# Expert layers with lists of 32 tokens on four strips of TensorE, and results returned through a DRAM table

## What is computed

```
def hier_moe(x, w_group, b_group, w_expert, b_expert, w1, w3, w2):
    ...
    weight = g_gate * e_gate
    expert_id = g_idx * MOE_EXPERTS_PER_GROUP + e_idx
    gates = jnp.sum(jax.nn.one_hot(expert_id, N_EXPERTS, dtype=f32) * weight[..., None], axis=1)

    def step(acc, ew):
        w1e, w3e, w2e, ge = ew
        h = jax.nn.silu(xt @ w1e) * (xt @ w3e)
        return acc + ge[:, None] * (h @ w2e).astype(f32), None

    y, _ = lax.scan(step, jnp.zeros((t, d), f32), (w1, w3, w2, gates.T))
```

## Time and profile before

| | |
|---|---|
| time, median of three runs | 2823.86 us |
| span of the profiled execution (first to last instruction) | 2819.0 us |
| median less span: what lies around | 4.9 us |
| TensorE busy | 2512.3 us, 89% of the span |
| VectorE, ScalarE, GpSimd busy | 800.3, 628.9, 164.9 us |
| bytes moved by DMA | 602.27 MB, mean 214 GB/s |
| MoE weights among them | 192 DMAs of 2 MB |
| chain that ended last | PE 70%, SP's queue 14%, DVE 6%, DMA 4% |

### The profile page before, as it was taken

One profiled execution on the slowest core, in us unless ns is written; L12 is line 12 of the kernel. 1 busy time (PEld: TensorE's weight loads), 2 busy tenths in 40 slices (PEclk: granted clock), 3 DMA queues, 4 the chain that ended last, 5 costly groups with the idle time before them and its releaser, 6 DMA issues.

```text
span 2819.0 us, 30761 instructions
## 1 busy us (share of the span) xinstructions
PE 2512.3 (89%) x12481; PEld 1598.0 (57%) x12482; DVE 800.3 (28%) x1338; ACT 628.9 (22%) x1012; POOL 164.9 (6%) x90
## 2 busy tenths in 40 slices
PE   7878999999979979999897897898999968878998
PEld 6544444444356644443333785556887847744996
DVE  1252011010020221011002546524232326354444
ACT  1121010101000610111102312423222224224334
POOL 0000000000000000000000325000000004240000
PEclk9988999999989989999999988899999988789999
DMA  8675976999966669999999001300323140130351
GB/s 326 260 276 187 393 286 231 393 393 394 396 250 243 233 242 385 394 393 393 395 396 359 1 1 60 123 1 22 113 90 120 45 163 1 60 117 7 135 199 71
DMA packets 241920, 602.27 MB, mean 214 GB/s; under 512 B 12679, under 2 KB 21751, under 8 KB 241824
## 3 DMA queue, kind: packets, MB, share of 16 engines
q1 hardware_dynamic: 241824, 600.91, 56.7%
HBM read 598.25 MB, written 2.64 MB: 213 GB/s over the span
## 4 chain that ended last, share of the span: by engine, by line
PE 70%; SPq 14%; DVE 6%; DMA 4%; ACT 2%; issue 2%; POOL 1%; DVEq 0%; ACTq 0%; POOLq 0%
PE ps L1756 13%; SPq L647 13%; PE ps L752 10%; PE ps L1565 8%; PE ps L1772 7%; PE ps L759 6%; PE ps L214 4%; PE ps L735 3%; PE ps L727 3%; PE ps L223 3%; PE ps L1738 3%; DMA ring<-in_moe_w_dram 1%; PE ps L1689 1%; PE ps L1709 1%; PE ps L313 1%
## 5 line engine op out<-in xcount | busy, mean ns | idle before, releaser
L752 PE MATMUL ps<-ring,arena 128*64 128x512 f32 x2176 | 477.2, 595 | 20.6 <-DMA ring<-in_moe_w_dram 18.7
L1756 PE MATMUL ps<-ring_r,ring_r 128*128 128x512 f32 (+1 forms) x2112 | 372.1, 339 | 12.5 <-DVE ring_r L2090 12.5
L1756 PEld LDWEIGHTS ps<-ring_r,ring_r 128*128 128x128 f32 x2112 | 329.0, 192 | 54.8 <-DVE ring_r L2090 13.1
L752 PEld LDWEIGHTS ps<-ring,arena 128*64 128x64 f32 x2176 | 155.9, 137 | 335.1 <-issue 305.8
L759 PE MATMUL ps<-ring,arena 128*64 128x512 f32 x1088 | 248.5, 598 | 26.8 <-ACT arena L817 13.8
L1565 PE MATMUL ps<-ring_r,ring_r 128*128 128x512 f32 (+2 forms) x1056 | 217.7, 367 | 8.9 <-DVE ring_r L1975 8.9
L1289 POOL TENSOR_TENSOR ring_r<-ring,ring_r 128x1024 fp32r<-128x1024 f32 (+2 forms) x28 | 85.9, 3088 | 2180.6 <-ACT ring_r L1284 2180.6
L1565 PEld LDWEIGHTS ps<-ring_r,ring_r 128*128 128x128 f32 x1056 | 189.1, 212 | 37.4 <-issue 9.3
L1772 PE MATMUL ps<-ring_r,ring_r 128*128 128x512 f32 x480 | 157.4, 401 | 12.3 <-DVE arena_r L1332 12.3
L759 PEld LDWEIGHTS ps<-ring,arena 128*64 128x64 f32 x1088 | 76.4, 137 | 151.2 <-issue 130.3
L907 DVE TENSOR_TENSOR arena<-ps,arena 128x512 f32<-128x512 f32 x34 | 23.6, 693 | 470.0 <-PE ps L752 470.0
(11 more groups left out here) (321 smaller groups left out, 2500.1 us busy)
## 6 DMA issues: line engine op xcount, KB each, us to landing
ring<-in_moe_w_dram SPq DMA_DIRECT2D x192, 2048.0 KB, 19.3
ring<-in_w_mod_dram SPq DMA_DIRECT2D x24, 2048.0 KB, 13.5
ring<-in_w_gate_dram SPq DMA_DIRECT2D x10, 2048.0 KB, 9.1
ring<-in_w_up_dram SPq DMA_DIRECT2D x10, 2048.0 KB, 14.2
ring<-in_w_in_dram SPq DMA_DIRECT2D x8, 2048.0 KB, 14.8
ring<-in_w_down_dram SPq DMA_DIRECT2D x8, 2048.0 KB, 11.4
ring<-in_w_out_dram SPq DMA_DIRECT2D x4, 2048.0 KB, 10.1
ring<-in_w_down_dram SPq DMA_DIRECT2D x4, 1536.0 KB, 8.1
```

The lines of the kernel that those rows point to most:

```text
L752: ins = pe.matmul(PS[CAP * e:CAP * e + CAP, 2 + c, :], xeT[:, k, CAP * e:CAP * e + CAP], w[c][:, e, k, :], start=(k == 0), stop=(k == KT - 1))
L1756: ins = pe.matmul(PS[:, 2 * (i % GU_BANKS) + a, 0:ntok], w[:, k, a, :], as_r(x[:, k, 0:ntok]), start=(k == 0 and n == 0), stop=(k == KT - ...
```

## The change

- CAP goes from 64 to 32 tokens of an expert in a round. In the up products each expert takes two strips of 32 columns of the array: one strip for the left half of the hidden width (`HALF` = 256 columns), one for the right. In the down product the two strips of an expert take the left and right 512 columns of the output. The loads of weights from DRAM are the same.
- Per round, PE's `scatter`, the transposes and copies of `selg`, and the product with the gates are gone. A round's result, 128 rows of 512 values (four strips: expert and half), is copied by DVE to `Y`, and ACT's queue sends it to a block of a table `y_rows` in DRAM, 256 KB a round (262,144 bytes). DVE's next copy to Y waits until this store has landed (`y_sent`).
- After the last round GpSimd (POOL) issues eight indirect DMAs a layer, each of 128 rows of 2 KB from the table, by row numbers that DVE has computed (`pick`): for both token tiles, both picks, both halves. DVE then forms wa * first + wb * second in four instructions, and the layer norm reads SBUF instead of PSUM.
- At the start of the program SP's queue writes zeros over the table (ten stores of 1 MB, from the memory of `O`), placed behind the load of da_wo and ahead of the store of the bias table, on whose landing the loads of the modulation weights wait.
- Ahead of the first round DVE computes the row numbers, after `ctrl` is written.

With the lists above, 34 rounds (18 and 16) become 43 (22 and 21): in layer 0 pairs 4, 5 and 6 take 3, 4 and 2 rounds where they took 2, 2 and 1.

The diff, cut to its core:

```diff
+    ROUNDS_MAX = 40
+    y_rows = nc.dram_tensor("y_rows", [ROUNDS_MAX * P, 512], F32)
...
+        sp.wait_ge(S("o_zero"), 1)
+        for n in range(ROUNDS_MAX // 4):
+            sp.dma_start(y_rows.ap()[4 * n * P:4 * (n + 1) * P, :].rearrange("(p a) d -> p (a d)", a=4), view(O[:, 0, 0:1], [1, 2048]))\
+              .then_inc(S("y_zeroed"), 16)
         sp.wait_ge(S("cc1"), 3)
         sp.dma_start(scratch.ap(), tab_sb).then_inc(S("tab_dma"), 16)
         sp.wait_ge(S("tab_dma"), 16)
...
+            if u == 0:
+                act.wait_ge(S("y_zeroed"), 16 * (ROUNDS_MAX // 4))
             act.wait_ge(S("values"), u + 1)
...
-    CAP = 64
+    CAP = 32
+    HALF = HIDDEN // 2
...
+        Yt = (ring[:, 3 * SLOT:3 * SLOT + 4096] if layer else arena[:, MARK:MARK + 4096]).rearrange("p (t n d) -> p t n d", t=NT, n=2)
...
+        cR, cB, cL = 50 * layer, 50 * layer + 16, 50 * layer + 33
...
-                    n_rounds = eng.value_load(ctrl[0:1, bass.ds(it * UNROLL + (cR + j), 1)], min_val=1, max_val=4)
+                    n_rounds = eng.value_load(ctrl[0:1, bass.ds(it * UNROLL + (cR + j), 1)], min_val=1, max_val=SEQ // CAP)
...
-            for b in range(4):
-                ins = pe.matmul(PS[:, 4 + b, :], zeros[:, 0:P], zeros, start=True, stop=False, skip_group_check=True)
-            ins.then_inc(s("sgT_ps"), 1)
-
-            def scatter(last=False):
-                for tt in range(NT):
-                    for h in range(2):
-                        ins = pe.matmul(PS[:, 4 + 2 * tt + h, :], sgT[:, tt * P:(tt + 1) * P], Y[:, h * 512:(h + 1) * 512],
-                                        start=False, stop=last, skip_group_check=True)
-                return ins
...
             def gather():
 
                 for k in range(KT):
                     for tt in range(NT):
-                        ins = pe.matmul(PS[:, 2 + k // 4, (k % 4) * P:(k % 4 + 1) * P], X[:, tt, k * P:(k + 1) * P],
-                                        view(sel[:, tt, 0, 0:1], [1, P]), start=(tt == 0), stop=(tt == NT - 1))
-                    if k % 4 == 3:
-                        ins.then_inc(s("xe"), 1)
+                        ins = pe.matmul(PS[:, 2, 2 * CAP * k:2 * CAP * (k + 1)], X[:, tt, k * P:(k + 1) * P],
+                                        view(sel[:, tt, 0, 0:1], [1, 2 * CAP]), start=(tt == 0), stop=(tt == NT - 1))
+                ins.then_inc(s("xe"), 1)
...
                         for e in range(2):
-                            ins = pe.matmul(PS[CAP * e:CAP * e + CAP, 2 + c, :], xeT[:, k, CAP * e:CAP * e + CAP], w[c][:, e, k, :],
-                                            start=(k == 0), stop=(k == KT - 1))
+                            for o in range(2):
+                                at = 64 * e + 32 * o
+                                ins = pe.matmul(PS[at:at + CAP, 2 + c, 0:HALF], xeT[:, k, CAP * e:CAP * e + CAP],
+                                                w[c][:, e, k, o * HALF:(o + 1) * HALF], start=(k == 0), stop=(k == KT - 1))
...
-                def down(h):
+                def down():
                     for k in range(4):
                         for e in range(2):
-                            ins = pe.matmul(PS[CAP * e:CAP * e + CAP, h, :], hT[:, k, CAP * e:CAP * e + CAP],
-                                            w[2][:, e, k, h * 512:(h + 1) * 512], start=(k == 0), stop=(k == 3))
+                            for o in range(2):
+                                at = 64 * e + 32 * o
+                                mid = 64 * e + 32 * (k // 2)
+                                ins = pe.matmul(PS[at:at + CAP, 0, :], hT[:, k % 2, mid:mid + CAP],
+                                                w[2][:, e, k, o * 512:(o + 1) * 512], start=(k == 0), stop=(k == 3))
                     return ins
...
-                pe.wait_ge(s("xe_act"), g + 1)
-                pe.wait_ge(s("xe_dve"), g + 1)
+                pe.wait_ge(s("xe_sb"), g + 1)
                 up(0)
                 up(1)
-                pe.wait_ge(s("y_act"), g + (1 + layer))
-                pe.wait_ge(s("y_dve"), g + (1 + layer))
-                scatter()
-                for tt in range(NT):
-                    ins = pe.transpose(PS[:, 0, tt * P:(tt + 1) * P], selg[:, tt, :], ident)
-                ins.then_inc(s("sgT_ps"), 1)
                 pe.wait_ge(s("h"), g + 1)
-                for k in range(4):
+                for k in range(2):
                     ins = pe.transpose(PS[:, 1, k * P:(k + 1) * P], hh[:, k * P:(k + 1) * P], ident)
                 ins.then_inc(s("hT_ps"), 1)
-                pe.wait_ge(s("sgT"), g + (2 + layer))
-                pe.wait_ge(s("hT"), g + 1)
-                arrived(2)
-                down(0)
                 pe.wait_ge(s("sel"), g + (2 + layer))
                 gather()
-                down(1).then_inc(s("y"), 1)
+                pe.wait_ge(s("hT"), g + 1)
+                pe.wait_ge(s("y_sb"), g + (1 + layer))
+                arrived(2)
+                down().then_inc(s("y"), 1)
             pe.wait_ge(s("ctrl"), layer + 1)
-            for b in range(2):
-                ins = pe.matmul(PS[:, b, :], zeros[:, 0:P], zeros, start=True, stop=True)
-            ins.then_inc(s("y"), 1)
+            pe.matmul(PS[:, 0, :], ident, cst[:, 0:512], start=True, stop=True).then_inc(s("y"), 1)
+            if layer == 0:
+                pe.matmul(PS[:, 2, :], ident, cst[:, 0:512], start=True, stop=True).then_inc(s("xe"), 1)
...
-            pe.wait_ge(s("y_act"), total + (1 + layer))
-            pe.wait_ge(s("y_dve"), total + (1 + layer))
-            scatter(last=True).then_inc(s("done"), 1)
+            pe.wait_ge(s("y_sb"), total + (1 + layer))
...
+            if layer == 0:
+                act.dma_start(y_rows.ap()[(ROUNDS_MAX - 1) * P:ROUNDS_MAX * P, :], cst[:, 0:512]).then_inc(s("y_sent"), 16)
...
-                act.wait_ge(s("xe"), g * 2 + (2 * layer + 1))
-                act.copy(view(xeT[:, 0, 0:1], [1, 512]), PS[:, 2, :]).then_inc(s("xe_act"), 1)
-                y_copy(g)
+                act.wait_ge(s("xe"), g + (layer + 2))
+                act.copy(view(xeT[:, 0, 0:1], [1, 512]), PS[:, 2, :]).then_inc(s("xe_sb"), 1)
+                at = act.value_load(ctrl[0:1, bass.ds(it * UNROLL + (cL + j), 1)], min_val=0, max_val=31 * P)
+                act.wait_ge(s("y_sb"), g + (1 + layer))
+                act.dma_start(y_rows.ap()[bass.ds(r * P + at, P), :], Y).then_inc(s("y_sent"), 16)
                 act.wait_ge(s("h1"), g + 1)
-                act.activation(hs, PS[:, 2, :], ACT.Silu).then_inc(s("silu"), 1)
-                act.wait_ge(s("sgT_ps"), g + (2 + layer))
-                act.copy(sgT, PS[:, 0, 0:256]).then_inc(s("sgT"), 1)
+                act.activation(hs, PS[:, 2, 0:HALF], ACT.Silu).then_inc(s("silu"), 1)
...
-                act.copy(view(hT[:, 0, 0:1], [1, 512]), PS[:, 1, :]).then_inc(s("hT"), 1)
-
-            def y_copy(g):
-
-                act.wait_ge(s("y"), g + (1 + layer))
-                act.copy(Y[:, 0:512], PS[:, 0, :]).then_inc(s("y_act"), 1)
+                act.copy(view(hT[:, 0, 0:1], [1, HALF]), PS[:, 1, 0:HALF]).then_inc(s("hT"), 1)
             for_rounds(act, body)
-            y_copy(act.value_load(ctrl[0:1, cB + PAIRS:cB + PAIRS + 1], min_val=1, max_val=128))
+            total = act.value_load(ctrl[0:1, cB + PAIRS:cB + PAIRS + 1], min_val=1, max_val=128)
+            at = act.value_load(ctrl[0:1, cL + PAIRS:cL + PAIRS + 1], min_val=0, max_val=32 * P)
+            act.wait_ge(s("y_sb"), total + (1 + layer))
+            act.dma_start(y_rows.ap()[bass.ds(at, P), :], Y).then_inc(s("y_sent"), 16)
...
-            link(dve.tensor_tensor(oh1, oh1, b2(wa, 32), ALU.mult))
-            link(dve.tensor_tensor(oh2, oh2, b2(wb, 32), ALU.mult))
-            link(dve.tensor_tensor(gates, oh1, oh2, ALU.add))
...
-            dve.tensor_copy(ctrl[:, cB:cB + 17], base).then_inc(s("ctrl"), 1)
+            link(dve.tensor_copy(ctrl[:, cB:cB + 17], base))
+            link(dve.tensor_scalar(blocks, base, base[:, 0:1], float(P), ALU.subtract, ALU.mult))
+            dve.tensor_copy(ctrl[:, cL:cL + 17], blocks).then_inc(s("ctrl"), 1)
+            link(dve.tensor_scalar(slot_of[:, 0:32:2], blocks[:, 0:16], float(P), None, ALU.add))
+            link(dve.tensor_scalar(slot_of[:, 1:32:2], blocks[:, 0:16], float(P + 64), None, ALU.add))
+            for n, oh in enumerate((oh1, oh2)):
+                link(dve.tensor_tensor(where, oh, view(slot_of, [0, NT], [1, 32]), ALU.mult))
+                link(dve.tensor_reduce(place[:, :, n:n + 1], where, AX.X, ALU.add))
+                link(dve.tensor_tensor(where, oh, rank, ALU.mult))
+                link(dve.tensor_reduce(turn[:, :, n:n + 1], where, AX.X, ALU.add))
+            link(dve.tensor_tensor(place, place, turn, ALU.add))
+            for m in range(1, SEQ // CAP):
+                link(dve.tensor_scalar(beyond, turn, m * CAP - 0.5, float(P - CAP), ALU.is_gt, ALU.mult))
```

(38 more changed lines are left out.)

31 lines of the change are left out of this document (12 added, 19 removed).

## The result

The changed kernel takes **2927.9 us**, median of four runs (2920.76 to 2935.03); the kernel before took 2824.58 beside it (2822.52 to 2826.35). The ratio is 1.0372, 95% interval [1.0354, 1.0389]: slower by 103 us. The forecast was slower by 47. The direction was right, but the measured change is more than twice the forecast one. The time lies in the stated range by luck: it is above the forecast's own range (2838 to 2905), which had been widened to 2945 for stores that wait behind the loads, and that is not what happened.

The account below looks back on a forecast made before the run. Weight loads, nearly level with PE, were taken to bound the expert loops. Zeros 11.2, layer 0 15.6 and layer 1 20.7 made 47.5 on a 2819.0 us span; with 4.9 for the median, 2871 us, range 2838 to 2945.

Parts of the forecast that it names:

- the forecast's own range: Whole kernel: 2838 to 2905 us, from varying the round, the gathers and the zeros; the forecast had chance 0.68.
- A pair takes 31.9 us and a faster PE meets a floor 2 us away.: Expert loops: loads need 31.9 us a pair, PE 29.75 a round, so a faster PE wins under 62 us.
- Sum: 16 us a round.: Expert loops: a new round's products, copies and selection add up to 16 us, within 15 to 17.5.
- Layer 0, "last w2 at 780.7": Layer 0's last weight landing: 780.7 against 778.0, with 44.8 us of stalls and 11.3 of Y stores.
- Layer 1, "no pair has over two rounds, so there is no stall": Layer 1's loop: no load stalls, 14.0 us for 21 stores, last w2 at 1522.5 against 1514.7.
- The start of a layer, 4.8 and 4.3: Before the first gather: DVE's added row-number steps delay it 4.8 us in layer 0, 4.3 in layer 1.
- The end of a layer, 12.9 each: Last w2 to layer norm: down, copy, store, gathers (16) and DVE sum to 30.1 us, against 17.2 before.
- The zeros, 11.2: Program start: 10.49 MB of zeros take 25.6 us and make the first modulation product wait 11.2 us.
- The queue rival: Y stores and gathers wait behind weight loads, lengthening layer ends and layer 0's additional rounds: 2945 us; chance 0.12.
- Stores beside loads at no cost: DMA engines: zeros and Y stores cost nothing beside loads, 2834.5 us, faster with short gathers; chance 0.07.
- Clock: PE's clock stays low between waits, also in rounds in a row: 26 us a round, 3016 us; chance 0.04.
- Strips not four abreast: Up and down products: the four strips don't run together, rounds stay at 26 us, 3016 us; chance 0.03.

Follow-up runs that it names:

- (4): Changed kernel without the store of Y in every round but a layer's last, so most of the result is missing: 2901.3 us, ratio 1.0269.
- rounds_as_before: Also (5): changed kernel with rounds counted as for lists of 64, 34 instead of 43, further entries left out: 2853.9 us, ratio 1.0110.
- pe_unrolled: Changed kernel with TensorE's loop over the pairs written out 16 times instead of 4: 2917.7 us, ratio 1.0324.
- pe_filler: Changed kernel with two unread 512-column matmuls in TensorE's loop, ahead of the wait for the next selection: 2924.6 us, ratio 1.0354.
- warm_start: Changed kernel with four unread products on TensorE between ctrl and each layer's first selection: 2928.2 us, ratio 1.0366.

## Why the prediction was half right

- **"A pair takes 31.9 us and a faster PE meets a floor 2 us away."** Right, and the reason for the direction. The DMA engines carried the same 192 loads at the same pace.
- **"Sum: 16 us a round."** Right inside a pair (15.47: 455.12 less 439.65 in the chain), wrong where a pair begins: 20 to 22 in a row of rounds (one of 16.9 where the clock stayed up), since DVE's selection comes 1.5 to 2 us late there and gather and down then mostly run at the low clock. The working had counted 1.75 us of DVE at a new pair, but not the clock behind the wait it makes.
- **Layer 0, "last w2 at 780.7".** The stalls behind pairs 4 and 5 were sized rightly (47.0 against 44.8). The stretch missed 14.6: loads resumed only at 278, 4 us late, since the first up ran slow; a stall behind pair 6 (4.5) that was excluded; pair 4 (2.5); and 5.8 MB of stores are 14.7 us at 394 GB/s, where I had 11.3. This is how the DMA engines' time was spent, not what each part costs: without the stores the layer was only 1.5 us shorter (4), and the long lists cost 50.0 (5) where I had 47.4, so 12 of the 14.6 us are there without them.
- **Layer 1, "no pair has over two rounds, so there is no stall": the step that failed.** Two rounds of 16 are 32 us, and the transfers of such a pair need 33.2 (31.9 and two stores), so by the sum a pair of two rounds just fits, and I took "just fits" for "never stalls". With 15.5 inside and 20 to 22 at the border such a pair takes 35 to 37. Twice two of them stand one behind the other, and at one border there are 6 us more at the loop's return. The loads stood 18.6 us instead of none, and resumed some 5 us later than forecast (1097 for 1091.6). rounds_as_before shows that the second rounds cost 20.8 us here, where I had 3.3, and pe_unrolled that 11.8 go when the waits at the loop's return do. What the low clock at the border costs by itself is not shown: pe_filler took it away, lengthened the rounds inside by 1.3 us and the waits at two of the returns to over 8, and won nothing. A lead of about a microsecond in a sum of five estimated terms is none: the forecast's own range had rounds of 17.5, and I should have run layer 1 through it too.
- **The start of a layer, 4.8 and 4.3.** Measured 8.1 and 7.2; the steps of DVE were right (5.9); the missing 3 are the gather at the low clock (7.09 for 3.8). warm_start has it at 3.79.
- **The end of a layer, 12.9 each.** Measured 15.4 and 14.8. The store of Y took 6.1 and 7.0, not 3.9: beside a full SP queue I had added too little. The gathers took 16.6 and 15.3 for 16, and down with the copy 4.7 for 5.8.
- **The zeros, 11.2.** Measured 14.2 and, alone, 15.1. Bytes right; again the low clock behind the wait (2.9).
- **The rivals.** The queue rival (Y lands behind the loads): no, 6.0 us against 19.8 for a weight load, two queues sharing; the rule of round-robin between queues, cited there from the Trainium skill ("DMA: Bandwidth & Descriptors"), agrees. Stores beside loads at no cost: no, 0.6 us each at pairs of one round (in layer 0 as a whole 1.5 us, which is within the scatter). Clock: half of it. From a pair's first up product to its last the products ran at full clock where TensorE had neither weights nor a loop's return to wait for; at new pairs gather and down ran slow, which the prediction had left out. Some 3 us at the first modulation product and at each layer's start are the clock's doing as well. Strips not four abreast: no, 64 records in 3.66 us.

At these three places I priced a product at the full clock and was low by about 3 us, each time because the change itself makes TensorE wait just ahead of it.

## What to carry over

Where loads set the pace and a ring gives little slack, cut a stage at the loads' rate, not at the engine's busy time, and run the list lengths through it: a pair whose rounds are reckoned at 96% of its transfers' time has no margin, and where two of them stood in a row, with 12 us of waits and slow products at the change, the loads stood for 12 us. Halving the capacity of a round was paid by the longest lists (74 of the 103 us), whatever the average list gained. The write to DRAM and the gather back cost the end of each layer 15 us, 7 of which went in layer 0 when fewer gathers ran without the next loads beside them; place them, and bytes such as the zeros, where the rate view shows the engines idle.

## What the runs showed of the hardware

- Behind short waits TensorE's next products were often slow: behind one of 1.93 us a gather of 32 records took 7.09 us in place of 3.79 (1333.17 above), and behind one of 11.73 us the first modulation product 6.54 in place of 3.66. Not each time: three gathers of the changed kernel behind waits of 1.51 and 1.52 us (at 333.15, 1234.21 and 1285.51) took 3.79. Spare products of 512 columns in the wait, two in the loop and four at a layer's start, kept most gathers at 3.7 to 3.8 (175.0 us for 45) and all down products at 3.64.
- TensorE showed waits of 4.4 to 5.1 us that no semaphore explains, behind a loop's return while the DMA engines were full, in layer 1 alone; sixteen bodies in place of four removed them. The DMA queue of instructions moved nothing in layer 0's loop and 32 packets of 16 KB in 490 us of layer 1's.
- GpSimd's indirect DMAs were issued each 1.25 us (0.95 busy), for rows of 2 KB and of 4 KB alike; with 256 KB each that is 210 GB/s, and beside full loads the eight took 16.6 us for 2 MB.
- A store of 256 KB on ACT's queue landed after 6.0 us (median of 45), most of them while SP's queue kept the DMA engines near 394 GB/s; its weight loads took 19.8.
